# In ff0, eight turnings of the hidden activations move from TensorE to VectorE and ScalarE

## The reference

```
def _swiglu(h, w_gate, w_up, w_down):
    return (jax.nn.silu(h @ w_gate) * (h @ w_up)) @ w_down
```

## Time and profile before

| what | value |
|---|---|
| median of 3 runs | 1618.78 us (1615.93 to 1619.92) |
| the profiled execution, its own time | 1621.67 us |
| its span, first to last instruction | 1620.0 us |
| mean granted TensorE clock | 0.997 of full speed |
| PE busy | 1593.2 us (98%) |
| DVE busy | 1097.9 us (68%) |
| ACT busy | 849.0 us (52%) |
| POOL busy | 558.2 us (34%) |
| bytes moved by DMA | 330.17 MB, 204 GB/s in the mean |
| ff0 (its bodies 1 to 10) | from about 177 to 352 us |

### The profile page before, as it was taken

One profiled execution on the slowest core, in us unless ns is written; L12 is line 12 of the kernel. 1 busy time (PEld: TensorE's weight loads), 2 busy tenths in 40 slices (PEclk: granted clock), 3 DMA queues, 4 the chain that ended last, 5 costly groups with the idle time before them and its releaser, 6 DMA issues.

```text
span 1620.0 us, 25097 instructions
## 1 busy us (share of the span) xinstructions
PE 1593.2 (98%) x9191; PEld 1323.2 (82%) x9191; DVE 1097.9 (68%) x1347; ACT 849.0 (52%) x1168; POOL 558.2 (34%) x886
## 2 busy tenths in 40 slices
PE   7999999999999999999999989999999999999999
PEld 4897788879877888788888978888888889888887
DVE  3888988889758765765657876555655556765554
ACT  2565533436655434576766665444544445664443
POOL 1102011000002564278964201555244643105553
PEclk9999999999999999999999999999999999999999
DMA  9976889874745765475654436656465655355652
GB/s 342 361 241 215 311 301 314 272 267 137 253 157 191 235 197 185 153 217 186 195 179 145 132 106 190 206 181 205 158 208 182 205 183 179 116 174 189 200 184 101
DMA packets 225918, 330.17 MB, mean 204 GB/s; under 512 B 10583, under 2 KB 187320, under 8 KB 225838
## 3 DMA queue, kind: packets, MB, share of 16 engines
q1 hardware_dynamic: 210480, 276.93, 52.4%
q0 software_dynamic: 14960, 52.06, 9.5%
q10 hardware_dynamic: 398, 0.11, 0.0%
HBM read 327.97 MB, written 1.09 MB: 203 GB/s over the span
## 4 chain that ended last, share of the span: by engine, by line
PE 90%; DVE 5%; ACT 2%; issue 1%; DMA 1%; SPq 0%; DVEq 0%; ACTq 0%
PE bank L2995 44%; PE bank L2719 26%; PE bank L2707 9%; PE bank L2677 3%; PE bank L2689 1%; DVE s_wL L2017 1%; PE bank L2829 1%; DMA s_late<-in_w_ada 1%; PE bank L2774 1%; PE bank L3007 1%; PE bank L2862 0%; ACT s_wH L1526 0%; PE bank L2845 0%; DVE s_x L2375 0%; DVE s_t L2360 0%
## 5 line engine op out<-in xcount | busy, mean ns | idle before, releaser
L2017 DVE TENSOR_TENSOR s_wL<-s_raw,s_wH 128x2048 fp32r<-128x2048 f32 x251 | 581.8, 2319 | 273.0 <-ACT s_wH L1526 272.3
L1526 ACT ACTIVATE s_wH<-s_raw 128x2048 fp32r<-128x2048 f32 x254 | 485.1, 1910 | 178.1 <-PE bank L2719 121.8
L237 POOL COPY s_mix<-s_mix 32x128 f32<-32x128 f32 x576 | 320.5, 556 | 378.5 <-DVE s_mix L2273 356.0
L2995 PE MATMUL bank<-s_wH,s_hH 128*128 128x512 f32 x1056 | 416.0, 394 | 3.4 <-DVE s_hL L2427 2.9
L2995 PE MATMUL bank<-s_wH,s_hL 128*128 128x512 f32 x1056 | 411.4, 390 | 0.0
L2995 PE MATMUL bank<-s_wL,s_hH 128*128 128x512 f32 x1056 | 411.2, 389 | 0.0
L2995 PEld LDWEIGHTS bank<-s_wH,s_hH 128*128 128x128 f32 x1056 | 198.2, 188 | 49.0 <-issue 5.8
L2995 PEld LDWEIGHTS bank<-s_wH,s_hL 128*128 128x128 f32 x1056 | 198.2, 188 | 41.8
L2995 PEld LDWEIGHTS bank<-s_wL,s_hH 128*128 128x128 f32 x1056 | 198.4, 188 | 40.4 <-issue 0.5
L2719 PE MATMUL bank<-s_wH,s_aH 128*128 128x512 f32 x496 | 194.3, 392 | 1.2 <-ACT s_gate L1534 1.0
L2719 PE MATMUL bank<-s_wH,s_aL 128*128 128x512 f32 x496 | 193.2, 389 | 0.0
(11 more groups left out here) (480 smaller groups left out, 2334.4 us busy)
## 6 DMA issues: line engine op xcount, KB each, us to landing
s_raw<-in_w_ffn_in SPq DMA_DIRECT2D x88, 512.0 KB, 5.0
s_raw<-in_ffn_w_gate SPq DMA_DIRECT2D x88, 512.0 KB, 3.9
s_raw<-in_ffn_w_up SPq DMA_DIRECT2D x88, 512.0 KB, 4.9
s_raw<-in_ffn_w_down SPq DMA_DIRECT2D x88, 512.0 KB, 4.2
s_late<-in_w_ada POOLq DMA_DIRECT2D x11, 2048.0 KB, 10.7
s_raw<-in_w_ffn_out SPq DMA_DIRECT2D x44, 512.0 KB, 4.4
s_late<-in_w_ada POOLq DMA_DIRECT2D x18, 1024.0 KB, 5.8
s_raw<-in_w_in_ab SPq DMA_DIRECT2D x24, 512.0 KB, 9.2
```

The lines of the kernel that those rows point to most:

```text
L237: return eng_copy(dst[32 * j:32 * j + 32, :, g, :], src[32 * g:32 * g + 32, :, j, :])
L1526: A(wH[:, slot, :], raw[:, slot, :], ACT.Copy).then_inc(hi_ready, 1)
L2017: TTn(wL[:, slot, :], raw[:, slot, :], wH[:, slot, :].bitcast(F32), ALU.subtract).then_inc(lo_ready, 1)
L2995: last = mm(bank[gu_bank(name, i, tt)][:], h, w[:, k, :], start=(half == 0 and k == 0 and j == 0), stop=(half == 1 and k == 3 and j == 2), ...
```

## The change

ff0 joins the layers that move, with ACT making the copies as in f1a. Bodies 1 to 8 are moved; body 0, body 9 and body 10 are turned on TensorE as before. The semaphore counts of the layers behind ff0 shift by eight. The blocks lie in `mix` from 9216 on, which is where ff1 has them.

```
-        SQUARES = {"ff1": 9216, "f1a": 4608, ...
+        SQUARES = {"ff0": 9216, "ff1": 9216, "f1a": 4608, ...
...
-        MOVED = {"ff1": 0, "f1a": 9, "f2a": 17, "f1b": 26, "f2b": 35}
+        MOVED = {"ff0": 0, "ff1": 8, "f1a": 17, "f2a": 25, "f1b": 34, "f2b": 43}
...
-            _turns += 3 if n == "f1a" else 2 if n in MOVED else FC
+            _turns += 3 if n in ("ff0", "f1a") else 2 if n in MOVED else FC
...
-                    elif name == "f1a":
+                    elif name in ("ff0", "f1a"):
                         moves(i)
...
-                    body(9, lambda r: r == 2 and ada_evac(0, 4, gdst=gate1[:, 1, 0:512], b=7))
+                    body(9, lambda r: r == 2 and ada_evac(0, 4, gdst=gate1[:, 1, 0:512], b=7), moved=False)
...
-                    body(9)
+                    body(9, moved=False)
...
-                    body(9, weights=(None, None, gate_rows))
+                    body(9, weights=(None, None, gate_rows), moved=False)
```

More of the change, by code:

```diff
@@ L148, in build_program @@
         tF = carve(mix, 1024, KC, T)
-        SQUARES = {"ff1": 9216, "f1a": 4608, "f2a": 4608, "f1b": 4608, "f2b": 4608}
+        SQUARES = {"ff0": 9216, "ff1": 9216, "f1a": 4608, "f2a": 4608, "f1b": 4608, "f2b": 4608}
         act_blocks = {n: mix[:, at:at + 512] for n, at in SQUARES.items()}
@@ L1717, in hidden @@
                 def hidden(i, dst):
-                    turns = i + 1 if name not in MOVED else 1 if i == 0 else i - 7 if name == "f1a" else 2
+                    turns = i + 1 if name not in MOVED else 1 if i == 0 else i - 7 if name in ("ff0", "f1a") else 2
                     act_e.wait_ge(act_tr, turns + TURNED[name])
```

## The result

The changed kernel takes 1622.02 us (median of 22 runs, 1619.69 to 1625.76), the kernel before 1619.88 us (22 runs, 1615.93 to 1622.12). The ratio is 1.0013, 95% interval 1.0007 to 1.0019: slower by some 2 us, where 1.6 us less was forecast. The profiled execution of the changed kernel has 1621.82 us and a span of 1620.1 us.

The account below looks back on a forecast made before the run. PE was taken to bound ff0, its end shared with DVE. 3.9 us taken from PE less 2.3 us of waits in body 10 left 1.6 us: 1617.2 us from the median 1618.78, range 1613.9 to 1620.8.

Parts of the forecast that it names:

- PE's 0.49 us a body: In ff0, removing four transposes from PE saves 0.49 us in each of eight bodies, 3.9 us in all.
- The ring: DVE and ACT waiting for each other in moved ff0 bodies: 16.62 us a body, longer than PE's new 16.32 us.
- Rivals B and C: In ff0: B, ring 0.5 us longer, 1621.2 us, chance 0.17; C, DVE's splits slow to 2.75 us, 1624.6 us, chance 0.05.
- Both move by 1.3 us and no more, if they take as long as before: The last piece's load and SP's load behind DVE's first split of body 9 come only 1.3 us earlier.
- I expect it to stay there, since the new waits are short: TensorE's granted clock stays at 1.00, its upper level of 2.4 GHz, despite new waits at ff0's end.
- The sum: 3.9 us taken from PE, 2.3 us given back as waits in body 10, 1.6 us left: 1617.2 us.
- The rule against the change: Skill's rule: transpose 128 × 128 on TensorE where PSUM will do as destination; by it nothing is won, 1618.8 us.

## Why the prediction was wrong, point by point

**PE's 0.49 us a body: right.** Seven bodies brought the norm 3.4 us nearer, five 2.3.

**The ring: right.** 16.62 us were forecast, 16.65 measured; the copies took 5.11 us, the splits 2.28 to 2.29, PE waited nowhere in bodies 2 to 8. DVE came to body 9 1.1 us earlier than in the profile that the forecast used, forecast 1.3. But in that profile it came late: its 134.29 stands against 133.42 and 133.78 in the two other profiles of this ff0, and between the means of three the gain is 0.6 us. Rivals B and C are refuted by these rows.

**"Both move by 1.3 us and no more, if they take as long as before": mis-sized.** The piece took 11.9, 11.6 and 10.7 us in three profiles of this ff0, against 10.7, 10.9 and 10.6 in three of that of before. In the first profile of the change it was issued 1.1 us earlier (325.06 − 184.79 against 327.38 − 186.02) and landed at the same distance, 152.1 to 152.2. So DVE came to the products of body 10 1.4 us later than forecast. PE reached `turn_act(10)` 0.4 us earlier than forecast, and waited 3.67 us instead of 1.8. In the profile with 10.7 us (body 8 written out) it waited 2.26. The transposes were forecast at a distance of 157.5 (343.5 − 186.02), and came at 159.0, 158.7 and 157.9: 1.1 us late in the mean.

**"I expect it to stay there, since the new waits are short": the step that failed.** The granted clock fell to 0.50 behind the waits of 3.67, 3.46, 3.26 and 2.26 us, and stayed at 1.00 behind 2.18 us and less. In the first profile of the changed kernel eleven matmuls at a distance of 0.43 us in place of 0.23 are 2.2 us; a part of that fills the wait for hL that PE would have had anyway. From the transposes to the norm the three profiles of the changed ff0 have 7.47, 6.50 and 6.48 us, against 5.68 where PE waits and the clock stays up: the fall cost 1.8, 0.8 and 0.8 us. Together with the load this takes all of the 1.6 us, and more. The Trainium skill, "TensorE: Matmul & The Clock Gate", section "What's actually happening", says that the lower clock is the default and that activity releases it. The rows agree: 0.50 behind an idle PE, 1.00 where fifteen matmuls of zeros fill the same gap. But the length of a wait alone doesn't decide. Here are the stall near 941 of the kernel with the piece in halves and the two stretches of 2 us around its end, and then the same stretches of the kernel before:

```profile
947.68 0.64 PE L502 MATMUL bank<-s_t,s_gate 128*32 128x64 f32 x28 [3.39 <-issue]
...
946.00:948.00 2.00, 0.32 (x23) 0.32 (x26) 1.87 (x4) 1.42 (x2) 0.00 (x0) 1.00 0.00 0
948.00:950.00 2.00, 2.00 (x42) 1.40 (x31) 1.79 (x1) 0.56 (x2) 0.00 (x0) 1.00 0.04 8
```

```profile
946.00:948.00 2.00, 2.00 (x45) 1.25 (x33) 1.99 (x1) 0.00 (x0) 0.00 (x0) 0.75 0.04 8
948.00:950.00 2.00, 2.00 (x20) 1.58 (x20) 0.30 (x1) 1.79 (x3) 0.00 (x0) 0.50 0.11 17
```

Behind 3.39 us the clock stayed at 1.00, behind 3.20 us it fell to 0.50. So these rows give no length of a wait by which the fall could be foretold.

**The sum.** Forecast was the norm 1.6 us earlier. Measured, it came 1.0 us later: 166.47, 165.24 and 164.40, mean 165.4, against 164.87, 164.00 and 164.36, mean 164.4. That is 2.6 us worse than forecast: 1.1 are the late transposes, 1.0 lie between them and the norm (6.8 in the mean, 5.8 forecast) and are the clock's, and 0.5 are the profile that the forecast started from, whose 164.87 is 0.5 above the mean. In the pair with body 8 written out the piece takes 10.6 and 10.7 us, the norm comes at 164.36 and 164.40, and the whole is 0.9994 and 0.9992: there neither the forecast's 1.6 us nor a loss is seen. Behind the norm, up to the first instruction that uses its scale, the changed kernel needs another 0.2 to 0.5 us (12.56 to 12.58 against 12.11 to 12.35). That makes 1.4 of the measured 2.1 us (interval 1.1 to 3.1); the rest I can't place. Of the 4.8 us between forecast and result, 1.1 are the base: the three runs shown had a median of 1618.78, 22 runs one of 1619.88.

**The rule against the change.** Taken alone it gave no gain, and the result is nearer to that than to my sum, but not for its reason: PE's work did shrink as the rows said, and with seven bodies moved the gain is there.

**The best version.** Seven moved bodies gain 0.30 to 0.33%, some 5 us. 3.4 of these are PE's transposes; against the kernel before in the same layout of PE's code (0.9994) it is 0.0025, 4 us. The rest comes with the place of the code. Why five bodies, 2.3 us nearer at the norm, measured no gain can be read in part from the three parts of the profiled spans:

| kernel | up to the steps ahead of body 1 | from there to the norm | behind the norm |
|---|---|---|---|
| before (two profiles) | 186.0, 185.1 | 164.9, 164.0 | 1269.1, 1269.1 |
| bodies 1 to 5 | 187.6 | 162.2 | 1269.5 |
| bodies 1 to 6 | 187.4 | 161.9 | 1266.7 |
| bodies 1 to 7 (two profiles) | 186.9, 187.0 | 161.1, 161.0 | 1266.7, 1266.8 |

Five bodies lose ahead of ff0 what they gain in it, and have the long part behind the norm; six and seven, with PE's code elsewhere, are 2.3 to 2.8 us shorter there. So most of the difference between five and six lies behind the norm and not in ff0. Up to 187 us the mean granted clock is 0.98 in the profiles with five, six and seven bodies, and 0.99 and 1.00 in the two of before. What makes that first part longer, and whether it belongs to these kernels or to the execution, stays open.

## What to carry to other kernels

When work leaves the engine that bounds, look for the first load that waits for the engine that got the work: the gain can end there, and one stage less of the move can be worth more than the last one. A new wait of TensorE costs its length and then, where the clock falls, what it takes from the matmuls behind it (here 0.8 to 2.0 us); price both. Compare kernels in which a loop turn is written out with a control of the same layout, since the code's place alone moved the time by 3.4 us in one kernel and by some 1 us, within the noise, in the other. And don't build a forecast of 1.6 us on the distances of one profile: to the norm, two profiles of the same program differ by 0.9 and by 1.2 us.

## What the hardware showed that I had not expected

- A 2 MB load that was issued 1.1 us earlier landed no earlier: 11.9 us in place of 10.7. With a loop turn of PE written out, and nothing else changed, it took 10.7 us again.
- The clock fell behind a wait of 2.26 us in one kernel, and stayed up behind 2.18 us in another, and in that other one also behind a stall of 3.39 us.
- Fifteen matmuls of zeros in the gap, 3.41 us, kept the clock at 1.00.
- PE stalled for 2.4 to 3.8 us within a run of small matmuls, with no releaser, at one place of the program; over 70 instructions more ahead of it took the stall away in three kernels and halved it in a fourth.
